# Stick-breaking decode attention: the suffix product and the weights of a group in four pieces of 512 keys, each in a step of its own

## The reference, cut to what matters

```
z = einsum('bqhd,bkhd->bhqk', q, k) * 64 ** -0.5 + sb_bias
mask = k_pos < q_pos
log_1mb = where(mask, log_sigmoid(-z), 0)
suffix = cumsum(log_1mb, reverse) - log_1mb
a = where(mask, exp(log_sigmoid(z) + suffix), 0)
o = einsum('bhqk,bkhd->bqhd', a, v)
```

## Time and profile before

| | us |
|---|---|
| median of 3 runs | 3236.05 (3235.11 to 3239.55) |
| the profiled execution | 3235.76 |
| its span, first to last instruction | 3234.1 |
| PE busy | 3165.6 (98%) |
| DVE busy | 2066.2 (64%) |
| ACT busy | 1653.5 (51%) |
| mean granted TensorE clock | 0.993 |

### The profile page before, as it was taken

How to read it: one execution, slowest core, us unless ns; L and a number is a source line. 1 busy time by engine, 2 the same in 40 slices (tenths; PEclk the granted TensorE clock), 3 DMA queues, 4 the chain that set the end, 5 groups by cost and what they waited for, 6 DMA issues and landing times.

```text
span 3234.1 us, 52008 instructions
## 1 busy us (share of the span) xinstructions
PE 3165.6 (98%) x18492; PEld 2926.4 (90%) x18492; DVE 2066.2 (64%) x2820; ACT 1653.5 (51%) x2375; POOL 149.1 (5%) x277
## 2 busy tenths in 40 slices
PE   8999999999999998999999999999999999999998
PEld 6888788787688877999999999999999999999998
DVE  4222322877887787776487755777567775678845
ACT  5443311887788776554354444445344553445433
POOL 0000000111311130000000000000000000000000
PEclk9999999999999999999999999999999999999999
DMA  5234334543644453534354433644336433444342
GB/s 172 93 97 135 87 114 117 146 125 99 206 116 122 118 167 109 156 115 118 110 165 132 117 115 103 188 119 116 109 107 182 122 115 114 138 131 117 112 121 76
DMA packets 577576, 406.03 MB, mean 126 GB/s; under 512 B 37977, under 2 KB 539138, under 8 KB 577378
## 3 DMA queue, kind: packets, MB, share of 16 engines
q1 hardware_dynamic: 536356, 301.45, 32.5%
q0 software_dynamic: 20544, 67.19, 7.2%
q10 hardware_dynamic: 20512, 35.17, 3.1%
HBM read 358.87 MB, written 44.87 MB: 125 GB/s over the span
## 4 chain that ended last, share of the span: by engine, by line
PE 60%; DVE 1%; DMA 0%; ACT 0%; issue 0%; DVEq 0%; ACTq 0%
PE pf_acc L60 20%; PE pf_acc L58 20%; PE pf_acc L59 19%; PE pf_ps_t L1578 1%; DMA ahead_mix<-XT 0%; PE pf_ps_sum L1517 0%; PE pf_ps_sum L1526 0%; PE pf_ps_sum L1531 0%; DVE pf_rs_sb L1898 0%; PE pf_ps_t L1588 0%; DVE pf_h L1866 0%; DVE pf_w_lo L1844 0%; DVE ahead_mix L1903 0%; DVE pf_f_lo L1914 0%; DVE pf_c L1928 0%
## 5 line engine op out<-in xcount | busy, mean ns | idle before, releaser
L1672 ACT ACTIVATE pf_w_hi<-ahead_raw 128x1024 fp32r<-128x1024 f32 x440 | 464.9, 1057 | 536.6 <-PE pf_acc L60 532.9
L58 PE MATMUL pf_acc<-pf_x_hi,pf_w_hi 128*128 128x416 f32 x2080 | 733.4, 353 | 2.2 <-DVE pf_h L1866 2.2
L60 PE MATMUL pf_acc<-pf_x_hi,pf_w_lo 128*128 128x416 f32 x2080 | 734.1, 353 | 0.0
L59 PE MATMUL pf_acc<-pf_x_lo,pf_w_hi 128*128 128x416 f32 x2080 | 726.0, 349 | 0.0
L1844 DVE TENSOR_TENSOR pf_w_lo<-ahead_raw,pf_w_hi 128x1024 fp32r<-128x1024 f32 x440 | 537.5, 1222 | 285.3 <-ACT pf_w_hi L1672 284.5
L58 PE MATMUL pf_acc<-pf_f_hi,pf_w_hi 128*128 128x416 f32 x1280 | 454.2, 355 | 9.4 <-DVE pf_f_lo L1911 7.2
L60 PE MATMUL pf_acc<-pf_f_hi,pf_w_lo 128*128 128x416 f32 x1280 | 452.1, 353 | 0.0
L59 PE MATMUL pf_acc<-pf_f_lo,pf_w_hi 128*128 128x416 f32 x1280 | 447.7, 350 | 0.0
L59 PEld LDWEIGHTS pf_acc<-pf_x_lo,pf_w_hi 128*128 128x128 f32 x2080 | 390.9, 188 | 7.9 <-issue 1.6
L58 PEld LDWEIGHTS pf_acc<-pf_x_hi,pf_w_hi 128*128 128x128 f32 x2080 | 390.4, 188 | 6.9 <-issue 4.9
L60 PEld LDWEIGHTS pf_acc<-pf_x_hi,pf_w_lo 128*128 128x128 f32 x2080 | 390.0, 187 | 2.3
(11 more groups left out here) (248 smaller groups left out, 4537.1 us busy)
## 6 DMA issues: line engine op xcount, KB each, us to landing
ahead_raw<-in_w_up_dram SPq DMA_DIRECT2D x220, 512.0 KB, 3.9
ahead_raw<-in_w_down_dram SPq DMA_DIRECT2D x80, 512.0 KB, 4.1
high_pages<-in_cache_k_dram POOLq DMA_DIRECT2D x128, 256.0 KB, 3.4
ahead_raw<-in_w_out_dram SPq DMA_DIRECT2D x40, 512.0 KB, 4.8
ahead_raw<-in_w_ple_gate_dram SPq DMA_DIRECT2D x40, 512.0 KB, 4.0
high_pages<-in_cache_v_dram POOLq DMA_DIRECT2D x64, 256.0 KB, 3.4
at_kT<-in_cache_v_dram POOLq DMA_DIRECT2D x64, 256.0 KB, 3.8
ahead_raw<-in_w_down_dram SPq DMA_DIRECT2D x40, 384.0 KB, 3.4
```

Source lines behind the costliest of these rows:

```text
L58: nc.tensor.matmul(out, stat_hi, mov_hi, start=first, stop=False)
L59: nc.tensor.matmul(out, stat_hi, mov_lo, start=False, stop=False)
L60: return nc.tensor.matmul(out, stat_lo, mov_hi, start=False, stop=last)
L1672: nc.scalar.activation(w_hi[k % 4][:, :], raw[k % 4][:, :], ACT.Copy).then_inc(hi_split, 1)
```

## The change

- One minus beta is no longer one instruction over 2052 columns at U_SCAN. There are eight over 256 columns, one for each pair of pages, in DVE's step two after the pair's logits (`sample_rest`), and one over the 4 new columns (`sample_last_rest`).
- U_SCAN and U_WEIGHT become four units, each in a step of its own. Piece n scans 512 keys, from the last piece to the first, beginning with the last value of the piece before, and then multiplies its own 512 columns (`sample_piece`). The last one also makes `a_new`.
- A group has 56 units in place of 54, so that the loop over `units_of` places other units too.
- The next group's queries are made at U_SUM + 8 in place of U_SUM - 1.

```diff
-    U_NEW, U_SCAN, U_WEIGHT, U_TURN, U_SUM = KEY_UNITS, KEY_UNITS + 1, KEY_UNITS + 2, KEY_UNITS + 3, KEY_UNITS + 5
+    PIECES = 4
+    U_NEW, U_SCAN, U_TURN, U_SUM = KEY_UNITS, KEY_UNITS + 1, KEY_UNITS + 1 + PIECES, KEY_UNITS + 3 + PIECES
...
-                    nc.vector.tensor_scalar(rest_s[:, :], beta_s[:, :], -1.0, 1.0, ALU.mult, ALU.add).then_inc(rest_made, 1)
-                    dve.wait_ge(rest_made, g + 1)
-                    r = rest_s[:, :][:, ::-1]
-                    nc.vector.tensor_tensor_scan(r, r, r, 1.0, ALU.mult, ALU.min).then_inc(scanned, 1)
-
-                def sample_weights(g):
-                    dve.wait_ge(scanned, g + 1)
-                    nc.vector.tensor_tensor(beta_s[:, 0:KEYS + 3], beta_s[:, 0:KEYS + 3], rest_s[:, 1:KEYS + 4], ALU.mult).then_inc(weighted, 1)
...
+                def sample_rest(g, pair):
+                    wait_emptied(dve, ("z", g, pair))
+                    cols = slice(2 * P * pair, 2 * P * (pair + 1))
+                    nc.vector.tensor_scalar(rest_s[:, cols], beta_s[:, cols], -1.0, 1.0, ALU.mult, ALU.add).then_inc(rest_made, 1)
...
+                def sample_piece(g, n):
+                    c0 = KEYS - (n + 1) * KEYS // PIECES
+                    c1 = c0 + KEYS // PIECES if n else KEYS + 4
+                    if n == 0:
+                        sample_last_rest(g)
+                    dve.wait_ge(rest_made, 9 * g + 9)
+                    if n:
+                        dve.wait_ge(scanned, PIECES * g + n)
+                    r = rest_s[:, c0:c1][:, ::-1]
+                    nc.vector.tensor_tensor_scan(r, r, r, rest_s[:, c1:c1 + 1] if n else 1.0, ALU.mult, ALU.min).then_inc(scanned, 1)
+                    dve.wait_ge(scanned, PIECES * g + n + 1)
+                    end = c1 if n else KEYS + 3
+                    done = nc.vector.tensor_tensor(beta_s[:, c0:end], beta_s[:, c0:end], rest_s[:, c0 + 1:end + 1], ALU.mult)
...
-                    if u == U_SCAN:
-                        sample_scan(g)
-                    if u == U_WEIGHT:
-                        sample_weights(g)
-                    if u == U_SUM - 1 and g + 1 < GROUPS:
+                    if U_SCAN <= u < U_TURN:
+                        sample_piece(g, u - U_SCAN)
+                    if u == U_SUM + 8 and g + 1 < GROUPS:
                         sample_queries(g + 1)
```

More of the change, by code:

```diff
@@ L895, in attend @@
         v_loaded, oT_stored, page_loaded = [front["v_loaded"], m.sem("v_loaded1")], join["oT_stored"], front["page_loaded"]
-        new_loaded, masks, blocks, new_masked, rest_made, scanned, weighted, owned, mix_stored = (
-            m.sem(n) for n in ("new_loaded", "masks", "blocks", "new_masked", "rest_made", "scanned", "weighted", "owned", "mix_stored"))
+        new_loaded, masks, blocks, new_masked, rest_made, scanned, weighted, piece_weighted, owned, mix_stored = (
+            m.sem(n) for n in ("new_loaded", "masks", "blocks", "new_masked", "rest_made", "scanned", "weighted", "piece_weighted", "owned", "mix_stored"))
         N_MASKS = 10
@@ L1318, in sample_queries @@
                     nc.vector.tensor_scalar(k_new[:, :, :], keep["kT_s"][:, :, cols], 1.0, None, ALU.mult).then_inc(blocks, 1)
-                def sample_scan(g):
-                    wait_emptied(dve, *[("z", g, pair) for pair in range(PAGES // 2)], ("new", g))
+                def sample_rest(g, pair):
+                    wait_emptied(dve, ("z", g, pair))
+                    cols = slice(2 * P * pair, 2 * P * (pair + 1))
+                    nc.vector.tensor_scalar(rest_s[:, cols], beta_s[:, cols], -1.0, 1.0, ALU.mult, ALU.add).then_inc(rest_made, 1)
@@ L1322, in sample_scan, with sample_last_rest @@
+                def sample_last_rest(g):
+                    wait_emptied(dve, ("new", g))
                     nc.vector.tensor_tensor(beta_s[:, KEYS:KEYS + 4], beta_s[:, KEYS:KEYS + 4], earlier[:, :], ALU.mult).then_inc(new_masked, 1)
                     dve.wait_ge(new_masked, g + 1)
-                    nc.vector.tensor_scalar(rest_s[:, :], beta_s[:, :], -1.0, 1.0, ALU.mult, ALU.add).then_inc(rest_made, 1)
-                    dve.wait_ge(rest_made, g + 1)
-                    r = rest_s[:, :][:, ::-1]
@@ L1327, in sample_scan @@
-                    nc.vector.tensor_tensor_scan(r, r, r, 1.0, ALU.mult, ALU.min).then_inc(scanned, 1)
-                def sample_weights(g):
-                    dve.wait_ge(scanned, g + 1)
-                    nc.vector.tensor_tensor(beta_s[:, 0:KEYS + 3], beta_s[:, 0:KEYS + 3], rest_s[:, 1:KEYS + 4], ALU.mult).then_inc(weighted, 1)
[L1332 to L1335, removed]
+                    nc.vector.tensor_scalar(rest_s[:, KEYS:KEYS + 4], beta_s[:, KEYS:KEYS + 4], -1.0, 1.0, ALU.mult, ALU.add).then_inc(rest_made, 1)
@@ new lines, in sample_piece @@
+                def sample_piece(g, n):
[11 more added lines that the diff above has]
+                    done = nc.vector.tensor_tensor(beta_s[:, c0:end], beta_s[:, c0:end], rest_s[:, c0 + 1:end + 1], ALU.mult)
+                    done.then_inc(piece_weighted, 1)
+                    if n == PIECES - 1:
+                        dve.wait_ge(piece_weighted, PIECES * (g + 1))
+                        nc.vector.tensor_tensor(a_new[:, :].rearrange("p (b t) -> p b t", b=PB),
+                                                beta_s[:, KEYS:KEYS + 4].unsqueeze(1).to_broadcast([P, PB, 4]),
+                                                row_seq[:, :].unsqueeze(2).to_broadcast([P, PB, 4]), ALU.mult).then_inc(weighted, 2)
@@ L1368, in _ @@
                         product(t - 1)
+                    for g, u in units_of[t - 2] if t > 1 else ():
+                        if u < KEY_UNITS and u % 4 == 3:
+                            sample_rest(g, u // 4)
                     for g, u in units_of[t]:
```

## The result

The median after the change is 3240.56 us (3238.67 to 3241.65), before it 3236.0 us (3234.14 to 3239.55): a ratio of 1.0013, 95% interval [1.0007, 1.0019]. The change costs 4.6 us, 0.14%: a small loss, clear of the noise of 20 runs, and less than the 0.2% that the forecast counts as no change.

The account below looks back on a forecast made before the run. PE, busy for 98% of the span, bounds the kernel, but DVE does in the two scan stretches. Group 0 -2.7, group 1 +3.3 and page units +1.0 give +1.6 us, so 3237.4 us; range 3231.0 to 3243.5 us.

Parts of the forecast that it names:

- The main thesis: Crowded stretches from U_NEW to first sums: no free DVE time to spread pieces into; chance 0.72, 3233 to 3242 us.
- The pieces: Scan stretch: four pieces at 1.90 us (1.22 and 0.68), pair's rest 0.27; 8.3 us in all against 8.2 before.
- the later start of the earlier placement: Group 0: key unit's logits in step 38 put step 39's scan at 767.5, 1.25 us later; group 1 0.4 us.
- The handover rule: DVE: 0.11 us per dependent handover, about five more in a group, already in the 1.90 us per piece.
- Group 0's scan and sums: Steps 40 to 48: copy into own at 817.4 us, block 2 of step 48 at 819.2; gain 2.7 us.
- The walk: Group 0's chain of times: step 39's scan at 767.5, copy at 817.4, PE reaching step 48 at 816.6 us.
- Group 1's scan and sums: Steps 109, 110: three sums in one step, copy at 1153.3 us, PE waits 2 to 3.5 us; loss 3.3 us.
- none over 3 us: Sign of being right: PE's waits for at_rest more in number, none over 3 us, total near before's.
- Page units: Steps with two key units, three heads with ten in their heavy half: loss 1.0 us, between 0 and 3.3.
- the second rival: ACT and the sums decide: extra key units in a head's steps 8 to 12; +7.3 us, 3243 us, chance 0.16.
- Queries: Moved from step 45 to 55: takes 1.7 us out of group 0's crowded stretch, costs nothing at i = 7.
- The sum: Whole kernel: -2.7 + 3.3 + 1.0 = +1.6 us, so 3237.4 us; own bounds 3233 to 3242 us.

Follow-up runs that it names:

- e1: Kernel before with two empty units, so every unit stands where the change puts it, scan whole: 3240.47 us, ratio 1.0016.
- e3: Changed kernel with the next group's queries back at U_SUM - 1 (step 46): 3240.65 us, ratio 1.0014.
- e7: Changed kernel with two pieces (placement of before), at most two early sums a step, queries at step 51: 3229.56 us, ratio 0.998.
- e11: Kernel before, scan whole, with at most two early sums a step and queries at step 51: 3230.31 us, ratio 0.9982.
- e12: Changed kernel with at most two early sums a step and every key unit in its step of before: 3228.93 us, ratio 0.9979.
- e4: Changed kernel with the next group's queries at U_SUM + 5 (step 51, i = 3): 3238.57 us, ratio 1.0009.
- e5: Kernel before with only the next group's queries moved to U_SUM + 5 (step 51): 3233.46 us, ratio 0.9993.
- e8: e7 with key units weighed 2.0 and 0.8 by group, group 0's pieces in steps 48 and 49, queries at U_MIX: 3239.45 us, ratio 1.0011.
- e10: e7 with key units weighed 1.6 and 0.9, group share 0.54, group 0's pieces in steps 50 and 51, queries at U_MIX: 3227.75 us, ratio 0.9973.

## Why the prediction was right, step by step

- **The main thesis held**: DVE has no free time between U_NEW and the first sums, so splitting spreads the waits and does not shorten their sum. Waits for `at_rest` rose from 9.7 to 12.7 us in sum, and 12.0 of that come with the placement alone (e1). e3 against e1 puts a price on four pieces and the rests, e7 against e11 on two: nothing within the measurement.
- **The pieces.** Taken 1.22 and 0.68 us, measured 1.26 and 0.69; the rest of a pair 0.27, measured 0.27. The scan of step 39 starts at 768.47, expected at 767.5: the later start of the earlier placement was under-sized by 1 us, part of the placement below.
- **The handover rule.** A piece's multiplication, which needs its scan, starts at 778.02, 0.04 us after that ends (776.72 + 1.26 = 777.98); the next instruction, which needs neither, starts at 778.63, 0.08 us before the end of the one in front (778.02 + 0.69 = 778.71). The Trainium skill, "VectorE: DVE Perf Modes", section on the DRAIN, would have the next operation wait for an empty pipeline and says that a semaphore adds nothing; it refers to a later section for operations that start earlier because nothing holds them. The early start of 0.08 us fits that exception, but the 0.12 us between the two kinds (0.11 in the prediction) is a price of the dependence, which the rule puts at zero. The measurement decides.
- **Group 0's scan and sums.** The waits of steps 43 to 45 were put at 1.6, 2.3 and 2.2 us and are 1.52, 2.08 and 1.92. The walk began 1.0 us late, at the scan of step 39, and is right from there on: the copy into `own`, at 817.4, came at 818.35, and block 2 of step 48, at 819.2, went at about 820.3 (the row of twelve transposes ends at 818.87 + 2.03 = 820.90, and the last four of them take 0.66 us). Against before that is a gain of 1.7 us where 2.7 were forecast. The table's 2.9 us is counted from step 42 on, behind the 1.4 us lost to the key units, and the forecast had 1.25 us of that in this walk; that 2.7 and 2.9 lie so close is luck. The wait of 2.5 us in step 48 came to 0.5 us, since PE reached the step at 818.87 and not at 816.6: 1.0 us by the late start, and most of the rest by a slow clock behind the wait of 1.92 us, which the sum did not have:

```profile
796.00:799.00 3.00, 3.00 (x14) 2.58 (x13) 3.00 (x2) 2.52 (x4) 0.00 (x0) 0.55 0.03 5
```

  It cost nothing in the end: without it PE would have stood in step 48 until the copy, as the walk had it.
- **Group 1's scan and sums.** Forecast a loss of 3.3 us, measured 4.3; the wait of 2.82 us at step 110 and its slow clock (0.69) came as foreseen. The copy came at 1156.55, 2.4 us of which is the lag brought along from the key units, which leaves 1154.2 against 1153.3: this 0.9 us is most of the miss. The wait of 3.15 us at 1118.46 breaks the forecast's "none over 3 us", with a slow clock behind it, but it is no loss against before, where the wait of 4.60 us a step later has the same clock behind it. After, then before:

```profile
1121.00:1124.00 3.00, 3.00 (x14) 2.61 (x13) 2.97 (x4) 2.25 (x3) 0.00 (x0) 0.50 0.88 204
```

```profile
1121.00:1124.00 3.00, 2.64 (x10) 2.45 (x11) 3.00 (x3) 1.09 (x2) 0.00 (x0) 0.50 0.55 167
```

  With 796 and 1158 us this makes three places with a slow clock in these stretches, one more than the forecast allowed itself; before the change there are three as well.
- **Page units.** Taken 1.0 us, measured 3.8, above the upper bound of 3.3 (e12 takes them away and has 0.0). This is the term that was most wrong. It was kept low "since PE is busy all the time in the same row", but that row ends ahead of the place where PE pays. The mechanism was the one of the second rival, ACT full from step 8 to 12 of a head, but it shows at another place: in the copy of a head's output (`join_oT`), which ACT reaches later and for which PE waits 0.4 to 1.0 us at a time, nine times in place of four; the five new ones stand in steps 16, 24, 64, 80 and 88, at i = 0 or 8. At step 76, with two key units, it waits 0.74 us for ACT's `at_kT`.
- **Queries.** Taken as free at i = 7, they cost 1.7 us. The step that failed is "at i = 7 DVE is idle in part": at 857 to 862 us DVE is busy for 4.78 of 5 us, and 1.7 us of copies in front of `weights` are 1.7 us of waiting for PE. It could have been read before: that stretch had DVE at 4.97 of 5 us with no queries in it. Before, then after:

```profile
857.00:862.00 5.00, 5.00 (x39) 3.61 (x37) 4.97 (x5) 5.00 (x10) 2.15 (x4) 1.00 0.92 257
```

```profile
857.00:862.00 5.00, 3.29 (x25) 2.78 (x24) 4.78 (x11) 3.47 (x7) 2.39 (x5) 1.00 1.02 227
```

  At i = 3 (e4, e5) the queries are free.
- **The sum.** Forecast +1.6 us; the terms measured give -2.9 + 4.3 + 3.8 + 1.7 = +6.9 us, of which 0.7 us is given back elsewhere in `attend` and 1.5 us behind it, where the kernels are the same, which leaves the 4.7 us of span. All the misses went towards a loss, in group 0 too when it is counted as the forecast did, and the second rival's sum, +7.3 us, was nearer to the trace of `attend` (+6.2 us) than the forecast. The median, +4.6 us, lies between the two. So the time fell into the range with the thesis right, but three of the sum's terms too low by 1.0 to 2.8 us, and the 1.5 us behind `attend` is luck.

## What to carry to other kernels

An engine that is busy for 64% of the span can have no free time in the one stretch that counts; splitting its work there moves no end. Moving the work to a stretch where it does idle gave a lead of 10.9 us at step 57 (e8), against 4.0 with the scan left in place (e7), but little of the difference reached the end: in e8 POOL's page issue set the pace next, and e10 is 1.8 us faster than e7. In a schedule written out by step, a change that adds steps moves all the other units: test the placement alone, with empty units. And count the fills that fall into one step against the banks of the ring: the third sum in a step, waiting behind a scan, was dearer here (3.0 us and 1.5 us of slow clock) than all the pieces.

## What the runs showed of the hardware that was not expected

Equal waits do not always bring the clock down. PE's wait of 2.81 us in step 43 was followed by 0.54 before the change; in e11 the same wait, to the hundredth, leaves the nine transposes at full speed, 1.20 us in place of 2.18:

```profile
779.79 1.20 PE L1049 MATMUL at_ps_t<-keep_ident,at_rest 128*128 128x128 f32 x9 [2.81 <-DVE at_rest L1293]
```

The granted clock from 780 to 783 us is 1.00 in e11. The stretch around the wait in step 110 shows the same pair, 0.69 after the change and 1.00 in e4. And length alone does not decide either: after the change a wait of 1.92 us was followed by 0.55. The Trainium skill, "TensorE: Matmul & The Clock Gate", Part 1, says that the number of matmuls at the low level differs from run to run of one kernel; these pairs are of two kernels each, so they agree with it but do not test it. What decides it after one of two equal waits stays open, as no run here separates that.

What a slow clock costs depends on who sets the pace. At step 110 it is 1.5 us. In step 43, where DVE is full, e11 is 1.3 us ahead of before behind the wait, and a step later level again: its PE waits 1.12 us for `weights` where the kernel before waits 0.25.
